# The last pair of experts: half of its scatter moved between the third and fourth quarter of its down projection

## The reference, cut to what matters

```
for l in range(DEPTH):
    xn = rms_norm(x, norm_mix[l])
    ... = split(xn @ w_in[l])             # latent attention, dilated attention, mLSTM
    x = x + concat([y_mla, y_dil, y_ml]) @ w_out[l]
    x = x + hier_moe(rms_norm(x, norm_ffn[l]), ...)

def hier_moe(x, ...):
    comb = weight of each expert for each token      # top 2 of the chosen group of 4
    h = silu(x @ w_gate[e]) * (x @ w_up[e]) * comb[e]
    return sum over e of h @ w_down[e]
```

## Time and profile before

| | |
|---|---|
| time, median of 3 runs | 1894.04 us (1892.47 to 1895.35) |
| the profiled execution, its own time | 1892.77 us |
| its span, first to last instruction | 1890.8 us |
| TensorE busy | 1838.9 us (97%) |
| VectorE busy | 740.3 us (39%) |
| ScalarE busy | 312.2 us (17%) |
| TensorE's mean granted clock | 0.992 of full speed |
| read from memory, whole span | 538.69 MB, 287 GB/s |

### The profile page before, as it was taken

How to read it: one execution, slowest core, us unless ns; L and a number is a source line. 1 busy time by engine, 2 the same in 40 slices (tenths; PEclk the granted TensorE clock), 3 DMA queues, 4 the chain that set the end, 5 groups by cost and what they waited for, 6 DMA issues and landing times.

```text
span 1890.8 us, 28374 instructions
## 1 busy us (share of the span) xinstructions
PE 1838.9 (97%) x12326; PEld 1417.3 (75%) x12326; DVE 740.3 (39%) x1545; ACT 312.2 (17%) x845; POOL 7.4 (0%) x15
## 2 busy tenths in 40 slices
PE   7999999999999999999899999999999999999998
PEld 6788887889866667656597888878888666667655
DVE  3477665567211221121236675655671121221112
ACT  2022222211211111011021131331121111111010
POOL 0000000000000000000000000000000000000000
PEclk9999999999999999999999999999999999999999
DMA  9342443137699999999794243341487999999995
GB/s 352 139 174 102 166 162 146 73 128 310 289 424 427 427 426 427 426 428 427 301 373 160 113 179 125 126 162 69 158 341 302 425 427 426 428 426 427 427 428 251
DMA packets 41712, 544.80 MB, mean 288 GB/s; under 512 B 4873, under 2 KB 5001, under 8 KB 7921
## 3 DMA queue, kind: packets, MB, share of 16 engines
q1 hardware_dynamic: 39600, 531.47, 67.9%
q0 software_dynamic: 1728, 11.42, 1.5%
q10 hardware_dynamic: 256, 0.04, 0.0%
HBM read 538.69 MB, written 4.22 MB: 287 GB/s over the span
## 4 chain that ended last, share of the span: by engine, by line
PE 96%; DVE 2%; issue 1%; DMA 1%; SPq 0%; ACT 0%; DVEq 0%
PE ps L756 93%; PE ps L810 1%; DMA ring<-in_w_lat 1%; PE ps L1209 1%; PE ps L826 0%; PE ps L915 0%; PE ps L818 0%; DVE PR L1863 0%; DVE ring L1757 0%; PE ps L1251 0%; DVE ring L1822 0%; PE ps L1125 0%; DVE v_mla L1986 0%; DVE scr L1955 0%; DVE ring L1767 0%
## 5 line engine op out<-in xcount | busy, mean ns | idle before, releaser
L756 PE MATMUL ps<-ring,scr 128*64 128x256 f32 (+2 forms) x3520 | 555.9, 425 | 6.6 <-issue 6.6
L756 PEld LDWEIGHTS ps<-ring,scr 128*64 128x64 f32 (+1 forms) x3520 | 316.9, 138 | 201.4 <-issue 112.8
L756 PE MATMUL ps<-ring,XN 128*128 128x256 f32 (+2 forms) x1184 | 244.1, 363 | 12.4 <-DMA ring<-in_w_lat 12.4
L756 PEld LDWEIGHTS ps<-ring,XN 128*128 128x128 f32 x1184 | 212.2, 191 | 33.1 <-issue 13.6
L756 PE MATMUL ps<-ring,X 128*128 128x256 f32 x896 | 200.6, 379 | 0.0
L756 PE MATMUL ps<-XN,ring 128*128 128x128 f32 (+1 forms) x1312 | 195.5, 306 | 0.9 <-DVE prob L1395 0.9
L756 PEld LDWEIGHTS ps<-XN,ring 128*128 128x128 f32 x1312 | 180.2, 192 | 13.7 <-issue 4.1
L756 PEld LDWEIGHTS ps<-ring,X 128*128 128x128 f32 x896 | 169.6, 190 | 22.7
L2028 DVE TENSOR_TENSOR v_mla<-scr,ps 128x256 f32<-128x256 f32 x32 | 13.5, 421 | 424.6 <-PE ps L756 424.6
L756 PE MATMUL ps<-BIAS,scr 128*64 128x256 f32 (+1 forms) x608 | 155.9, 414 | 5.0 <-issue 5.0
L756 PE MATMUL ps<-PR,scr 128*64 128x256 f32 (+2 forms) x576 | 160.0, 434 | 0.7 <-DVE scr L2039 0.3
(11 more groups left out here) (271 smaller groups left out, 1478.9 us busy)
## 6 DMA issues: line engine op xcount, KB each, us to landing
ring<-in_moe_w_up SPq DMA_DIRECT2D x44, 2048.0 KB, 22.5
ring<-in_moe_w_down SPq DMA_DIRECT2D x44, 2048.0 KB, 26.5
ring<-in_moe_w_gate SPq DMA_DIRECT2D x42, 2048.0 KB, 24.3
ring<-in_w_main SPq DMA_DIRECT2D x36, 2048.0 KB, 9.2
ring<-in_w_out_a SPq DMA_DIRECT2D x16, 1280.0 KB, 5.8
PR<-in_moe_w_down SPq DMA_DIRECT2D x10, 2048.0 KB, 24.0
XN<-in_moe_w_gate SPq DMA_DIRECT2D x10, 2048.0 KB, 27.9
BIAS<-in_moe_w_up SPq DMA_DIRECT2D x10, 2048.0 KB, 23.2
```

Source lines behind the costliest of these rows:

```text
L756: return pe.matmul(o, lhsT, rhs, start=start, stop=stop, skip_group_check=True)
```

## The change

TensorE scatters `sc0` to `sc3` of pair 7 between its quarters `dy2` and `dy3`, after waiting for the copies of `dy0`, `dy1` and `Sw`; `sc4` to `sc7` follow `dy3` and the branch, each two behind the copy of the quarter that they need. VectorE adds `sc0` to `sc3` between its copies of `dy1` and `dy3`. In layer 0, the blocks of `sc0` to `sc3` are scaled into `XN` where they were, behind the branch; ScalarE's scaling waits for `dy3` as well. It holds for both layers.

```diff
@@ TensorE, in the loop over pairs
                         for q in range(2):
                             name = f"dy{2 * half + q}_{i}"
+                            if (half, q, i) == (1, 1, NE // 2 - 1):
+                                pe.wait_ge(*copied(f"sw_{i}", l))
+                                for n in range(2):
+                                    pe.wait_ge(*copied(f"dy{n}_{i}", l))
+                                scatter(i, range(KT // 4))
                             pe.wait_ge(*freed(name, l))
@@ TensorE, behind the sweep
-                written(NE // 2 - 1)
-                scatter(NE // 2 - 1, range(KT // 2))
+                for n in (2, 3):
+                    pe.wait_ge(*copied(f"dy{n}_{NE // 2 - 1}", l))
+                    scatter(NE // 2 - 1, (2 * n, 2 * n + 1))
@@ VectorE, in the loop over pairs
                         dve.tensor_copy(Y[:, n * 512:(n + 1) * 512], bank(f"dy{n}_{i}")[0:2 * CAP, :]).then_inc(*read(f"dy{n}_{i}"))
+                        if (n, i) == (1, NE // 2 - 1):
+                            add_moe(i, range(KT // 4))
@@ VectorE, behind the sweep
                 for k in range(KT // 2):
-                    add_moe(NE // 2 - 1, (k,))
+                    if k >= KT // 4:
+                        add_moe(NE // 2 - 1, (k,))
                     if l + 1 < DEPTH:
                         dve.wait_ge(*copied(f"sc{k}_{NE // 2 - 1}", l))
                         gained(2 * k, l + 1)
@@ ScalarE, behind the sweep
                 if l + 1 < DEPTH:
+                    act.wait_ge(*ready(f"dy3_{NE // 2 - 1}", l))
                     for k in range(KT // 2):
```

More of the change, by code:

```diff
@@ L1273, in _ @@
                     i = NE // 2 - 1
-                    for name in [f"sc{k}_{i - 1}" for k in range(KT // 2)] + [f"sw_{i}"] + [f"dy{n}_{i}" for n in range(4)]:
+                    for name in [f"sc{k}_{i - 1}" for k in range(KT // 2)] + [f"sc{k}_{i}" for k in range(KT // 4)] + [f"sw_{i}"] + [f"dy{n}_{i}" for n in range(4)]:
                         pe.wait_ge(*copied(name, l))
```

## The result

The changed kernel took 1898.21 us (median of 20 runs, 1896.26 to 1904.29) against 1893.14 us (20 runs) before. The ratio is 1.0035, 95% interval 1.0027 to 1.0043: 6.6 us slower, 5.1 to 8.1 (the two medians alone lie 5.1 us apart). Forecast were 1894.2 us and no difference that can be told, so the prediction was wrong: the time lies above its range, and the change is slower by more than what was called the bound. The profiled execution took 1897.01 us.

A forecast was written before the change was run, and what follows sets the result against it. TensorE, busy 97% of the span, was taken to bound the kernel. Layer 0's +1.15 and layer 1's -1.02 gave +0.13 on 1892.77, so 1892.9; medians run 1.27 higher, hence 1894.2 us, range 1891.3 to 1897.1.

The forecast's parts named there:

- what was called the bound: Whole kernel: 0.2%, 3.8 us, as the least difference a measurement can tell from no change.
- The stop behind `dy3` goes, 1.06 and 0.99 us saved: End of both layers: `sc4` and `sc5` hide the copy of `dy3`, saving 1.06 us in layer 0, 0.99 in layer 1.
- The branch, as a rival: Behind `dy3`: TensorE's flag loads and jump show; at the bound layer 1 gains nothing, 1895.2 us; chance 0.12.
- What it takes no row shows: Flag loads and jump behind `dy3`: unlisted time, bounded by TensorE's restart to within 1.06 and 0.99 us.
- Layer 1, -1.02 us: End of layer 1: the last addition starts at 1885.93 instead of 1886.95, 1.02 us earlier.
- The two first ones leave earlier, which nothing waits for: End of layer 1: the first two output writes leave earlier, without effect; the last follows as before.
- Layer 0, +1.15 us: End of layer 0: `c0`'s load is issued 3.46 us later, so `c0` starts at 952.01 instead of 950.86.
- wait for the load +2.24: Layer 0, ahead of `c0`: 2.24 us of idle time, with the load taken to land 5.6 us after issue.
- `c0`'s second half would cause no wait: Layer 0: the second half lands at 953.70, needed at 954.6, 0.9 us to spare.
- The clock: Behind `c0`'s longer idle time TensorE runs partly at 1.2 GHz, losing 1.6 us: 1895.8 us; chance 0.16, 0.08 for slower.
- a case at 1898.5 us: Larger clock loss, 2.0 and 1.3 us, on top of +1.15 without layer 1's gain: +4.4 us; slower, chance 0.08.
- The time that it gives for a load between the two, "1892.5": Layer 0: `c0`'s load takes the page's 3.8 us, between the hidden load and 5.6 us; whole kernel 1892.5 us.

The follow-up runs named there:

- the short body: Changed kernel with TensorE's slow-path body left out save for its last wait, flag loads and branch kept: 1.0004 to the kernel before.
- +3.6 (1.3 to 5.7, alone): The change made in layer 1 only, layer 0 as before but for ScalarE's wait: 1.0019 to the kernel before.
- first experiment: Changed kernel without flag wait, flag loads, branch and slow-path body on all engines: 0.9994; the kernel before without them: 1.0000.
- the early loads: Changed kernel with TensorE's flag wait and loads moved behind `ht0` of pair 7, branch left in place: 1.0001 to the kernel before.
- the few waits: Changed kernel with the bank waits of `sc0` to `sc3` moved ahead of `dy0` and `dy2`: one profiled execution, no ratio; stops 2.04 and 2.60 us.
- the full product: Kernel before with one added product of 128 weight columns, waiting for its bank, between `dy2` and `dy3` of pair 7: 1.0020.
- the last version: Kernel before with the scatter whole behind the branch, its copy waits split, and flag wait and loads behind `ht0` of pair 7: 0.9989.
- the half product: Kernel before with one added product of 64 weight columns, waiting for its bank, between `dy2` and `dy3` of pair 7: 1.0019.

## Why the prediction was wrong

*The stop behind `dy3` goes, 1.06 and 0.99 us saved:* this step failed. The prediction named the copy as what TensorE waited for, since the earlier trace rows name it, and let the scatter's second half hide it. That part held: `sc4` did not wait for the copy (the stop is "issue" now). But the jump ended there within 0.4 us of the copy, and the move made TensorE reach it 0.8 us later and, in layer 1, take longer over it: the stops measured 1.82 and 2.66 us.

*The branch, as a rival:* right in its mechanism, wrong in its bound, and given 0.12. The prediction said that what the branch takes was over within 1.06 and 0.99 us, since TensorE was back by then. That bounds how much of it lies behind `dy3`'s end, and only for that order of instructions; it was taken as a bound of its whole length. "What it takes no row shows" holds for the rows printed there, not for the trace: the branch alone took 3.34 and 3.37 us. The chain in fact begins 4.2 us ahead of `dy3`'s end, with the fetch 1.8 to 2.0 us ahead of it, and restart comes 2.5 to 3.3 us behind the fetch. When the fetch's lead fell to 0, 2.66 us stood in the open. The rule that was weighed there (the Trainium skill, Runtime: NRT & Kernel Launch, Instruction fetch mechanics) is what the short body and the instruction queue's packets bear out: a branch of 0.2 us without a packet, of 3.3 to 4.0 with one. VectorE shows what loads and jump take on an engine for which no packet was seen: 1.47 us between the copy of `dy3` and its first scaling in the changed kernel, 0.07 of it the branch.

*Layer 1, -1.02 us:* measured +3.7 (profile) and +3.6 (1.3 to 5.7, alone). Without the slow path it was -0.7, so the sum of the prediction was right to 0.3 us for a kernel without a jump. "The two first ones leave earlier, which nothing waits for", it said of the output writes; nothing does, but the flag's loads and the branch ran beside them and took 1.2 us longer than before.

*Layer 0, +1.15 us:* measured +1.10, by another way. The terms were: stop -1.06, wait for the load +2.24. What happened: stop +0.76, passages between quarters and scatter +0.3, no wait. The load took 4.4 us, not 5.6, and without the stop (first experiment) TensorE waited 1.14 us for it. So "+2.24" was mis-sized by a factor of two, and hidden on top. The right number was luck. That `c0`'s second half would cause no wait held in the changed kernel; with the early loads it cost 0.72 us.

*The clock:* the rival's mechanism came, in layer 1 rather than at `c0`, at 1.7 us. It fell behind the stops of 2.6 us in four profiles of five (2.66, 2.61, 2.63 and 2.65, not the 2.60 of the few waits) and behind the 2.27 and 1.95 of the full product, but not behind 2.07, 2.04 or 1.82 elsewhere. So no length of the stop decides it here. That its cause is the stop is inferred: where the stop was gone, or 0.51 us, the four banks took 3.7 us.

*The range:* its upper end, 1897.1, allowed one mishap. Two came together, and if the longer stop brought the clock with it, they were not independent. The prediction had itself a case at 1898.5 us (clock, 0.08 for slower) and left it outside its range. The time that it gives for a load between the two, "1892.5", should by its own terms be 1892.4.

*Left open:* why the loads are reached 0.6 to 0.8 us later once something stands between `dy2` and `dy3`; the first table rules out waits and the number of small products, not more. Whether added instructions shift where the jump's target lies in what is fetched was not tested; the branch's length in the kernels with the order of before or with small products varies from 3.3 to 3.8 us. And whether the output writes are what lengthens loads and branch in layer 1. Of the two comparisons, 5.5 us (3.8 to 7.2) holds the 4.8 of the profile, and 6.6 (5.1 to 8.1) just misses it; the profile is one execution.

## What to carry to other kernels

A stop that the profile puts down to one releaser may have a second cause of the same length behind it; before counting its whole length as gain, ask what else the engine does there, jumps and register loads above all. The chain and the timeline leave them out, but the trace has them: ask it for the source line of the branch and of the flag's load. Packets in the instruction queue beside the engine's restart are a second trail. A branch over a long body that never runs held TensorE's sequencer for over 3 us here: load its condition well ahead, and leave a long unbroken run of queued products in front of it, as the last version did. And a write that "nothing waits for" can still run beside something that matters.

## What the runs showed of the hardware that was not expected

- On TensorE, a jump over some 245 products fetched a block of 0.02 MB about 1.0 to 1.7 us after the branch began; the branch took 3.3 to 4.0 us, and TensorE was back 2.5 to 3.3 us after the fetch where nothing else held it. A jump over two instructions fetched nothing, took 0.2 us and left no stop. VectorE's took 0.07 us.
- TensorE's sequencer reached the loads behind `dy3` 4.2 us before `dy3`'s end, 3.6 or 3.4 us once a single product stood between two quarters. A product that lengthened its piece by 0.2 or 0.6 us made the kernel 3.7 us slower (1.7 to 5.7), of which the profile with the half product explains 1.9.
- The same register load took 0.31 us with idle DMA engines in layer 1, and 0.90 us with output writes running.
- The same load of 768 KB landed 5.6 us after its issue before, and 4.4, 4.7 and 4.2 us in three later kernels, from idle DMA engines each time.
